# GpSimd makes the context's half of the conditioning sums during the first projection

## The reference, cut to what matters

```python
def ada_modulation(cond, w, b):
    m = jax.nn.silu(cond) @ w + b
    return jnp.split(m[..., None, :], N_MOD, axis=-1)

sh_a, sc_a, g_a, sh_m, sc_m, g_m = ada_modulation(c, w_ada[layer], b_ada[layer])
csh_a, csc_a, ...               = ada_modulation(c_ctx, w_ada[layer], b_ada[layer])
h  = modulate(rms_norm(x, norm_attn_w[layer]), sh_a, sc_a)
hc = modulate(rms_norm(ctx, norm_attn_w[layer]), csh_a, csc_a)
```

## Time and profile before

| | |
|---|---|
| median of 3 runs | 2277.32 us |
| profiled execution, its own time | 2285.57 us |
| its span, first to last instruction | 2283.9 us |
| TensorE matmul busy | 2182.5 us, 96% |
| VectorE busy | 1521.3 us, 67% |
| ScalarE busy | 1064.6 us, 47% |
| GpSimd busy | 135.2 us, 6% |
| chain that ended last | TensorE 93%, ScalarE 3%, VectorE 2% |
| first projection, first ada instruction to last matmul | 30.6 to 208.7 us |

### The profile page before, as it was taken

The page is one execution under the profiler, slowest core; times in us unless marked ns, Lnnn a source line. Parts: engine busy times, 40 slices in busy tenths (PEclk is TensorE's granted clock), DMA queues, the critical chain, the costliest instruction groups (busy, mean ns, idle before and its releaser), DMA issues.

```text
span 2283.9 us, 30297 instructions
## 1 busy us (share of the span) xinstructions
PE 2182.5 (96%) x10232; PEld 1807.2 (79%) x10232; DVE 1521.3 (67%) x1845; ACT 1064.6 (47%) x1379; POOL 135.2 (6%) x233
## 2 busy tenths in 40 slices
PE   7999998999999999999978999889999999999997
PEld 6888776788778888888867778777888888888876
DVE  6987788687895887768665364556655555655655
ACT  5444654555433554345456355345434434444442
POOL 2101000101010101100000000001000000000000
PEclk9998999999998999999999999899999999999999
DMA  8985077788786888977645250465756756766652
GB/s 283 305 292 188 1 233 263 231 267 267 254 281 207 276 273 276 310 247 240 205 147 184 86 184 1 147 203 192 232 185 211 240 193 211 233 199 205 222 182 94
DMA packets 267022, 482.51 MB, mean 211 GB/s; under 512 B 14861, under 2 KB 107349, under 8 KB 265633
## 3 DMA queue, kind: packets, MB, share of 16 engines
q1 hardware_dynamic: 236544, 367.18, 48.1%
q0 software_dynamic: 30192, 113.72, 15.8%
q10 hardware_dynamic: 176, 0.08, 0.0%
HBM read 478.81 MB, written 2.11 MB: 211 GB/s over the span
## 4 chain that ended last, share of the span: by engine, by line
PE 93%; ACT 3%; DVE 2%; issue 1%; DMA 0%; DVEq 0%; ACTq 0%
PE G L1416 28%; PE G L1418 28%; PE G L1417 28%; PE T L1463 1%; PE T L1600 1%; PE T L1709 1%; PE T L1452 1%; PE T L1541 1%; ACT junk L498 1%; PE G L1689 1%; ACT w_hi L548 1%; PE G L1534 1%; PE T L1564 0%; DVE h_lo L941 0%; PE G L1730 0%
## 5 line engine op out<-in xcount | busy, mean ns | idle before, releaser
L868 DVE TENSOR_TENSOR w_lo<-raw,w_hi 128x1024 fp32r<-128x1024 f32 x696 | 844.0, 1223 | 481.3 <-ACT w_hi L548 477.0
L548 ACT ACTIVATE w_hi<-raw 128x1024 fp32r<-128x1024 f32 x696 | 735.4, 1060 | 913.5 <-PE G L1418 911.1
L1416 PE MATMUL G<-w_hi,h_hi 128*128 128x512 f32 (+1 forms) x1920 | 754.6, 393 | 17.1 <-ACT w_hi L548 7.1
L1418 PE MATMUL G<-w_hi,h_lo 128*128 128x512 f32 (+1 forms) x1920 | 749.4, 390 | 0.0
L1417 PE MATMUL G<-w_lo,h_hi 128*128 128x512 f32 (+1 forms) x1920 | 749.3, 390 | 0.0
L1416 PEld LDWEIGHTS G<-w_hi,h_hi 128*128 128x128 f32 x1920 | 363.9, 190 | 95.1 <-issue 11.3
L1418 PEld LDWEIGHTS G<-w_hi,h_lo 128*128 128x128 f32 x1920 | 363.6, 189 | 75.3
L1417 PEld LDWEIGHTS G<-w_lo,h_hi 128*128 128x128 f32 x1920 | 363.8, 189 | 72.9
L1416 PE MATMUL G<-w_hi,a_hi 128*128 128x512 f32 x896 | 353.4, 394 | 5.6 <-ACT w_hi L548 4.2
L1418 PE MATMUL G<-w_hi,a_lo 128*128 128x512 f32 x896 | 350.8, 392 | 0.0
L1417 PE MATMUL G<-w_lo,a_hi 128*128 128x512 f32 x896 | 350.7, 391 | 0.0
(11 more groups left out here) (233 smaller groups left out, 1173.2 us busy)
## 6 DMA issues: line engine op xcount, KB each, us to landing
ada_w<-in_w_ada POOLq DMA_DIRECT2D x192, 512.0 KB, 5.0
raw<-in_w_up SPq DMA_DIRECT2D x176, 512.0 KB, 6.0
raw<-in_w_mlp_up SPq DMA_DIRECT2D x128, 512.0 KB, 4.7
raw<-in_w_mlp_down SPq DMA_DIRECT2D x128, 512.0 KB, 4.7
raw<-in_w_in SPq DMA_DIRECT2D x104, 512.0 KB, 5.2
raw<-in_w_down SPq DMA_DIRECT2D x88, 512.0 KB, 5.9
raw<-in_w_out SPq DMA_DIRECT2D x64, 512.0 KB, 4.8
raw<-in_w_in SPq DMA_DIRECT2D x8, 272.0 KB, 4.1
```

The costliest lines, as they stand in the source:

```text
L548: act.activation(w_hi[:, s % 4], raw[:, s // 2 % 4, STEPK * (s % 2):STEPK * (s % 2) + STEPK, :], ACT.Copy).then_inc(hi_ready, 1)
L868: dve.tensor_tensor(w_lo[:, s % 4], raw[:, s // 2 % 4, STEPK * (s % 2):STEPK * (s % 2) + STEPK, :], w_hi[:, s % 4].bitcast(F32), ALU.subtr ...
L1416: pe.matmul(out, ah, wh, start=f, stop=False)
L1418: mm = pe.matmul(out, al, wh, start=False, stop=l)
```

## The change

The context's instruction leaves VectorE's list. GpSimd makes the same product and sum in two instructions: a `tensor_scalar` (half tile times one number per partition) into the scratch `u_buf`, and a `tensor_tensor` that adds it to the accumulator. Its loop over the half tiles is written out, and before each fetch stands the context's work on the buffer that the fetch will overwrite. GpSimd waits for each of its own results by a new semaphore, `ada_pooled`. TensorE waits for all 64 of them before it sums the accumulators.

```diff
+    ada_pooled = sem("ada_pooled")
...
             if run == 0:
+                def context(t, half):
+
+                    pool.wait_ge(ada_full[half], t * 16 + 16)
+                    part = u_buf[:].rearrange("p b n -> p (b n)")
+                    pool.tensor_scalar(part, ada_w[:, half, :], silu[:, 1, t:t + 1], None, ALU.mult).then_inc(ada_pooled, 1)
+                    pool.wait_ge(ada_pooled, t * 4 + 2 * half + 1)
+                    pool.tensor_tensor(ada_acc[:, 1, half, :], ada_acc[:, 1, half, :], part, ALU.add).then_inc(ada_pooled, 1)
+                    pool.wait_ge(ada_pooled, t * 4 + 2 * half + 2)
+
                 tile(0, 0, None)
                 tile(0, 1, None)
-                with pool.Fori(1, count // 2) as t:
-                    tile(t, 0, t * 2 - 1)
-                    tile(t, 1, t * 2)
+                pool.wait_ge(ada_used, 1)
+                for t in range(1, count // 2):
+                    for half in range(2):
+                        context(t - 1, half)
+                        tile(t, half, t * 2 - 1 + half)
+                context(count // 2 - 1, 0)
+                context(count // 2 - 1, 1)
...
                     half = (k // 2) % 2
                     dve.wait_ge(ada_full[half], 16 + i * 32 + 16 * (k // 4))
-                    for c in range(2):
-                        ins = dve.scalar_tensor_tensor(out=ada_acc[:, c, half, :], in0=ada_w[:, half, :],
-                                                       scalar=silu[:, c, bass.ds(i * 2 + k // 4, 1)],
-                                                       in1=ada_acc[:, c, half, :], op0=ALU.mult, op1=ALU.add)
-                    ins.then_inc(ada_used, 1)
+                    dve.scalar_tensor_tensor(out=ada_acc[:, 0, half, :], in0=ada_w[:, half, :],
+                                             scalar=silu[:, 0, bass.ds(i * 2 + k // 4, 1)],
+                                             in1=ada_acc[:, 0, half, :], op0=ALU.mult, op1=ALU.add).then_inc(ada_used, 1)
                     dve.wait_ge(ada_used, i * 4 + k // 2 + 1)
...
             pe.wait_ge(ada_used, ADA_END[q])
             if q >= 1:
                 pe.wait_ge(ada_col, q)
+            if q == 0:
+                pe.wait_ge(ada_pooled, 2 * ADA_RUNS[0][2])
```

## The result

The changed kernel takes 2318.87 us, the median of 4 runs (2318.6 to 2325.73), against 2279.47 of the kernel before (4 runs, 2276.34 to 2283.1). The ratio is 1.018, 95% interval 1.0154 to 1.0205: slower by 39 us. Forecast was 2330, and taking turns at SBUF as the cause. The direction and the size hold.

A forecast was written before the change was run, and what follows sets the result against it. TensorE was taken to bound the first projection; SBUF turns would stretch its 32 periods from 5.44 to 7.0 us, moving its end from 208.7 to 262.2, +53.5 us. On the 2277.3 us median that gave 2330, range 2274 to 2360.

The forecast's parts named there:

- TensorE as the bound: In the first projection TensorE already runs at its undisturbed pace, 178 products in 40 us; VectorE is close behind.
- The removal: 32 instructions leaving VectorE, 40.9 us, gain only 1.2 us, at the first projection's start where TensorE waits for a w_lo.
- Turns at SBUF: First projection: VectorE and GpSimd block each other's SBUF reads, period 7.0 us instead of 5.44, +53.5 us; chance 0.50.
- GpSimd by itself would be hidden: First projection: without contention, GpSimd's series of 4.3 us per half tile fits the 5.44 us period.
- rival 2: First projection: no contention, but GpSimd's series is the bound; with a 4.0 us sum +28 us, 2305; chance 0.06.
- The end: End of the first projection: TensorE's new wait, and GpSimd's memset and fetch of tab1, stay hidden unless the stage lengthens.
- Rival 4: First projection: turns, and TensorE's clock falls for half of the time; +92 us, 2369; chance 0.06.

The follow-up runs named there:

- e1: Kernel before plus a tail after the output is stored, GpSimd and VectorE instructions alone, then together; alone the product takes 2.84 us, the sum 2.34, the copy 1.04.
- e6: Changed kernel with a one-column memset in place of GpSimd's sum, so only the product is made; 2280.83 us, ratio 1.0013.
- e4: Changed kernel with a one-column memset in place of GpSimd's product, so the half tile is summed unscaled; 2297.59 us, ratio 1.0088.
- e7: Changed kernel, but GpSimd takes the context's half of every second half tile only and VectorE keeps the other; 2296.54 us, ratio 1.0081.
- e3: Changed kernel with GpSimd's product and sum replaced by three memsets, which read nothing; 2307.93 us, ratio 1.0126.
- e5: Changed kernel with GpSimd's product replaced by a copy of the half tile, the sum kept; 2324.69 us, ratio 1.0204.
- e2: Kernel before, but VectorE leaves out the context's half in the first projection and GpSimd only fetches; 2276.74 us against 2278.65, ratio 0.9989.

## Why the prediction was right, and where not

| kernel | GpSimd's series | turns, from e1 | period measured | ratio |
|---|---|---|---|---|
| before | short | 5.1 | 5.44 (TensorE) | 1 |
| product only (e6) | 3.9 | 4.6 | 5.44 (TensorE) | 1.0013 |
| sum only (e4) | 3.4 | 5.9 | 5.94 | 1.0088 |
| half (e7) | short | 5.9 | 5.88 | 1.0081 |
| memsets (e3) | 6.4 | none | 6.38 | 1.0126 |
| changed | 6.2 | 6.7 | 6.53 | 1.018 |
| copy and sum (e5) | 4.4 | 6.7 | 6.68 | 1.0204 |

All in us per half tile. The series is GpSimd's instructions alone, end to end with its 0.3 and 0.6 for the fetch; e7 is per half tile, half of 11.75. The measured period is near the longest of three: TensorE's 5.44, the series, the turns. In the changed kernel it is 0.2 under the turns from e1, since its own trace has 0.7 us of VectorE per product and 2.0 per sum, which makes 6.5.

- *What bounds the kernel, and what the removal is worth.* TensorE as the bound is right. The removal gave 1.9 us by the medians (e2; between 5.5 less and 0.5 more), forecast 1.2. The forecast read the wrong row for it: the 3.5 us wait of the earlier trace rows is not the one behind the ada instructions, which was 2.14. That one did become 1.2 us shorter. Left out were the 9 products at the lower clock after it, another 1.7 us.
- *Turns at SBUF.* Right as a mechanism, shown by e1, e4, e5 and e7. The term was mis-sized: I had 3.73 for VectorE, 3.14 for GpSimd and 0.12 for two changes of hands, 7.0; e1 gives 3.63 + 2.9 + 0.13 = 6.7, and the changed kernel runs at 6.53. The sum was near (2.34 alone, 2.1 of it held, for 2.09). The product was off twice: 2.84 instead of 1.05 alone, but holding VectorE back for only 0.8. In the total these errors nearly cancelled, and that was luck. 32 periods shorter by 0.5 us are 15 us, and 53.5 - 15 = 38.5 is close to the 39 us by the medians. The profiled execution lost 41.6 up to the end of in1: with periods of 6.53 the same sum puts the last product at 247.2, it came at 250.25, and the difference is mostly the slow start (28.8 us for four half tiles instead of 26.1).
- *"GpSimd by itself would be hidden."* Wrong. I took the product at the copy's 1.05. With 2.84 and 2.34 the series is 6.2 us undisturbed (2.84 + 0.1 + 2.34 + 0.3 + 0.6), over TensorE's 5.44, and e3 shows a series of 6.4 costing 29 us. The term that failed is this price. Such a series was rival 2, for which I asked a product and sum above 4.3 us together: they are 5.2. I gave it 0.06 and looked for the excess in the sum. The nearest row to a product was a copy, and it was no measure.
- *Which of the two it is in the changed kernel.* Each alone costs 29 or 45 us, together 39, so they don't add: two limits of nearly the same height. GpSimd's timeline has no wait for VectorE and VectorE's hardly one for GpSimd's half tiles (5.0 us in six waits, 4.2 of it before 51 us), which is how such a tie looks. Taking away the length and keeping the reads returned nothing (e5). Taking away the reads and keeping the length returned 11 us (e3); its series is 0.2 us longer than product and sum undisturbed, so a return of some 17 us is my estimate for undisturbed ones, which no run made.
- *The end.* The new wait was hidden, as forecast, and the memset and the fetch behind it cost nothing. GpSimd's last product and sum do cost a little, for they lie over the last w_lo: from the last ada instruction's end to the end of in1 it is 11.2 us instead of 9.8.
- *The clock.* Rival 4 didn't come as a rule of the stage: from 62 to 235 us the granted clock is 1.00 with gaps of 0.8 us in each period. It came in small at the start, where the window from 40 to 80 us has 0.91: after waits of 2.2 and 3.4 us some 17 products ran 0.43 us apart (from 47.72 and from 58.41). From 200 to 240 us it was 0.96.

The Trainium skill (SBUF — State Buffer, Who interferes with whom) has the later of the two block until the first has finished. For the sum and for VectorE's instructions this case's runs agree (2.1 us of a sum of 2.34; nothing for memsets, nothing with PSUM). For the product they don't: it held VectorE for 0.8 of 2.84 us, and e6 ran 32 of them with TensorE at its full 178 products in mid stage. The Trainium skill (GPSIMD Engine Reference, When to use GPSIMD) calls one-input work there roughly line-rate; the copy fits that (1.04 us for 1024 elements, where VectorE's w_lo takes 1.22), the product doesn't (2.84), and the measurement decides.

## What to carry to other kernels

Before work moves from VectorE to GpSimd, ask two things apart: does GpSimd's whole series per period fit, with the product priced from a product and not from a copy, and do both engines' SBUF reads fit into the period together. Here VectorE's one instruction of 1.3 us became 2.9 us of shared reading, so each half tile moved made VectorE's line longer by 1.6 us instead of shorter. Here TensorE was the bound as well, so even a clean removal (e2) gave 2 us. Such a move could pay only where VectorE is the bound and GpSimd's reads fall beside instructions that they don't hold; no run here has such a case. When a trace after shows one engine never waiting and the other with longer instructions, replace the suspect by work of the same length that doesn't read (e3) and by work that reads as much in less time (e5): the two together show whether one limit or two stand there.

## What the runs showed of the hardware

GpSimd's product of 1024 floats by a factor takes 2.84 us, its copy 1.04, its sum of two 2.34; 512 elements of the product take 1.56 us. A GpSimd read costs a VectorE instruction with two SBUF inputs 0.8 us per 1024 elements for one input and 2.1 for two, even where the GpSimd instruction itself lasts much longer; beside w_lo without a pause the product takes 4.15 us and the sum 3.20. GpSimd memsets (0.95 us) and VectorE's w_lo don't disturb each other, nor do GpSimd's sums and VectorE instructions with one input in PSUM. A `tensor_scalar` of 2 elements with one SBUF input took 2.06 us under a GpSimd sum, 0.17 without. TensorE kept its full clock with a gap of about 0.8 us in every 6.5. At the start of the stage the products behind a wait of 2.1 us (at 34.47, kernel before) and of 3.4 us (at 58.41, changed kernel) ran at the lower level, 9 and 8 of them.
